# Pairs of squares added on POOL before PE sums them over the features

## The reference

```python
def rms_norm(x, gain=None):
    xf = x.astype(jnp.float32)
    y = xf * lax.rsqrt(jnp.mean(xf * xf, axis=-1, keepdims=True) + RMS_EPS)
...
h = rms_norm(x, norm_g[l, 0]) * (1.0 + sc1) + sh1
```

## Time and profile before

| | us |
|---|---|
| median of 3 runs | 1771.9 (1767.98 to 1773.8) |
| the profiled execution's own time | 1766.4 |
| its span | 1764.4 |
| PE busy | 1561.6 (89%) |
| PE weight loads busy | 1506.8 (85%) |
| DVE busy | 1077.8 (61%) |
| ACT busy | 716.1 (41%) |
| POOL busy | 277.4 (16%) |

### The profile page before, as it was taken

One profiled execution on the slowest core, in us unless ns is written; L12 is line 12 of the kernel. 1 busy time (PEld: TensorE's weight loads), 2 busy tenths in 40 slices (PEclk: granted clock), 3 DMA queues, 4 the chain that ended last, 5 costly groups with the idle time before them and its releaser, 6 DMA issues. The chain is left out here.

```text
span 1764.4 us, 27370 instructions
## 1 busy us (share of the span) xinstructions
PE 1561.6 (89%) x11950; PEld 1506.8 (85%) x11950; DVE 1077.8 (61%) x1279; ACT 716.1 (41%) x797; POOL 277.4 (16%) x221
## 2 busy tenths in 40 slices
PE   2897689999898689999897685999989998899999
PEld 2886589999787589999897584999989997899998
DVE  6765757787455448688474633576895443456444
ACT  2533345433542445533474411433334443343332
POOL 0000200053000001044000111010253700300012
PEclk7998779999798579999798885899998999889999
DMA  9570549787140228888243001378893542436650
GB/s 395 224 262 1 207 187 350 291 332 291 72 160 32 76 92 320 324 308 333 99 170 117 1 1 35 146 281 303 312 354 144 189 173 93 143 129 229 217 211 29
DMA packets 47207, 336.71 MB, mean 191 GB/s; under 512 B 5360, under 2 KB 5744, under 8 KB 6768
## 3 DMA queue, kind: packets, MB, share of 16 engines
q1 hardware_dynamic: 46224, 333.09, 50.7%
q10 hardware_dynamic: 864, 1.87, 0.3%
HBM read 333.89 MB, written 1.05 MB: 190 GB/s over the span
## 5 line engine op out<-in xcount | busy, mean ns | idle before, releaser
L417 DVE TENSOR_TENSOR weights_hi_lo<-ring,weights_hi_lo 128x2048 fp32r<-128x2048 f32 x213 | 514.5, 2417 | 399.2 <-ACT weights_hi_lo L411 398.4
L411 ACT ACTIVATE weights_hi_lo<-ring 128x2048 fp32r<-128x2048 f32 x213 | 407.4, 1914 | 638.8 <-PE PS L519 347.1
L519 PE MATMUL PS<-hi,weights_hi_lo 128*128 128x256 f32 x3200 | 526.9, 288 | 25.5 <-DVE weights_hi_lo L417 17.1
L519 PEld LDWEIGHTS PS<-hi,weights_hi_lo 128*128 128x128 f32 x3200 | 451.3, 195 | 29.4 <-DVE weights_hi_lo L417 19.1
L789 PE MATMUL PS<-acts_hi_lo,weights_hi_lo 128*128 128x256 f32 x3552 | 446.3, 288 | 33.9 <-DVE weights_hi_lo L417 21.1
L789 PEld LDWEIGHTS PS<-acts_hi_lo,weights_hi_lo 128*128 128x128 f32 x3552 | 439.2, 196 | 41.3 <-DVE weights_hi_lo L417 25.0
L519 PE MATMUL PS<-lo,weights_hi_lo 128*128 128x256 f32 x1600 | 326.7, 286 | 0.0
L519 PEld LDWEIGHTS PS<-lo,weights_hi_lo 128*128 128x128 f32 x1600 | 253.8, 195 | 0.0
L428 DVE CUSTOM_DVE_ANT_0 ring<-ring,cond 128x1024 f32<-128x1024 f32 x192 | 248.4, 1333 | 1.0 <-DMA smallS<-in_small_dram 0.9
L737 POOL CAST acts_hi_lo<-arena 128x512 fp32r<-128x512 f32 x74 | 73.8, 998 | 993.6 <-PE PS L789 538.2
L519 PE MATMUL PS<-weights_hi_lo,hi 128*128 128x256 f32 x1248 | 203.2, 284 | 9.2 <-DVE weights_hi_lo L417 8.0
(11 more groups left out here) (325 smaller groups left out, 1100.4 us busy)
## 6 DMA issues: line engine op xcount, KB each, us to landing
ring<-in_stream_dram SPq DMA_DIRECT2D x313, 1024.0 KB, 4.9
constS<-in_const_dram SPq DMA_DIRECT2D x1, 1856.0 KB, 11.3
cond<-in_rows_dram SPq DMA_DIRECT2D x2, 512.0 KB, 6.0
arena<-in_x_dram ACTq DMA_DIRECT2D x1, 1024.0 KB, 12.5
smallS<-in_small_dram SPq DMA_DIRECT2D x1, 883.0 KB, 12.4
out_dram<-arena ACTq DMA_DIRECT2D x2, 256.0 KB, 2.5
out_dram<-arena SPq DMA_DIRECT2D x2, 256.0 KB, 2.9
constS<-in_const_dram SPq DMA_DIRECT2D x1, 320.0 KB, 13.0
```

The source lines that it names most:

```text
L411: act.activation(wsp[:, g % 2, 0, :], ring[:, n % RING, :], ACT.Copy).then_inc(*hi_ready.one())
L417: dve.tensor_tensor(wsp[:, g % 2, 1, :], ring[:, n % RING, :], wsp[:, g % 2, 0, :].bitcast(F32), ALU.subtract).then_inc(used["dve"], 1)
L519: mm = pe.matmul(o, lhs, rhs, start=k + g + j == 0, stop=k == KD - 1 and j == 2, skip_group_check=True)
```

## The change

POOL gets a part in each group of sums (`pair_squares`): for each of the three units of two tiles it waits for the squares and adds the second tile's 256 columns to the first's, in place, in float32. PE (`unit_sums`) waits for that sum in place of the squares, and multiplies only the first 256 columns by the ones: two matmuls for each unit, ten in a group for sixteen. The units of one tile are summed as before. In the start phase and in the output and down projections POOL's part stands behind the work that it had there. New signals `x_squares_paired` and `y_squares_paired` order it. The rest of the diff, left out below, removes signals that no instruction used.

```diff
--- before.py
+++ after.py
@@ -32,6 +32,7 @@
 EARLY_CONST = 266
 MOD_COLS = 40
 UNITS = ((0, 1), (2, 3), (4, 5), (6,), (7,))
+PAIRS = 3
 
 
 IN = {}
@@ -583,13 +584,21 @@
             state["taken"] = [bank_taken(i) for i in range(n_pe)]
             close()
 
-        def unit_sums(pe, u, sq, bank, ready, done):
-
-            pe.wait_ge(*ready.at(u + 1))
-            for c in range(len(UNITS[u])):
-                for m in range(TT):
-                    mm = pe.matmul(PS[:, bank, m:m + 1], sq[:, u % 2, c * SEQ + m * P:c * SEQ + (m + 1) * P], ones[:, 0:1],
-                                   start=u + c + m == 0, stop=u == len(UNITS) - 1, skip_group_check=True)
+        def pair_squares(pool, sq, squared, added):
+
+            for u in range(PAIRS):
+                pool.wait_ge(*squared.at(u + 1))
+                pool.tensor_tensor(sq[:, u % 2, 0:SEQ], sq[:, u % 2, 0:SEQ], sq[:, u % 2, SEQ:2 * SEQ], ALU.add).then_inc(*added.one())
+
+        def unit_sums(pe, u, sq, bank, squared, added, done):
+
+            if u < PAIRS:
+                pe.wait_ge(*added.at(u + 1))
+            else:
+                pe.wait_ge(*squared.at(u + 1))
+            for m in range(TT):
+                mm = pe.matmul(PS[:, bank, m:m + 1], sq[:, u % 2, m * P:(m + 1) * P], ones[:, 0:1],
+                               start=u + m == 0, stop=u == len(UNITS) - 1, skip_group_check=True)
             mm.then_inc(*done.one())
 
         def spread(pe, r, bank, ready, done):
@@ -607,14 +616,14 @@
             sq = area(TEMP_AT, 2, 512)
             tmp, r = spare[:, 0:1024].rearrange("p (i t) -> p i t", i=4), stat[:, 48:50]
             R = PS[:, 2, 0:SEQ]
-            xsq, xsum, xrt, xr, rx, td, hd, ld = (sig(n) for n in (
-                "x_squares", "x_square_sums", "x_roots", "x_rstd", "x_rstd_spread", "x_scaled", "h_hi_ready", "h_lo_ready"))
+            xsq, xad, xsum, xrt, xr, rx, td, hd, ld = (sig(n) for n in (
+                "x_squares", "x_squares_paired", "x_square_sums", "x_roots", "x_rstd", "x_rstd_spread", "x_scaled", "h_hi_ready", "h_lo_ready"))
             state["h_hi"] = [hd.at(k + 1) for k in range(KD)]
             state["h_lo"] = [ld.at(k + 1) for k in range(KD)]
 
             def pe_part(pe):
                 for u in range(len(UNITS)):
-                    unit_sums(pe, u, sq, 0, xsq, xsum)
+                    unit_sums(pe, u, sq, 0, xsq, xad, xsum)
                 spread(pe, r, 2, xr, rx)
 
             def act_part(act):
@@ -645,7 +654,10 @@
                         dve.scalar_tensor_tensor(lo[:, k - 1, :], tmp[:, (k - 1) % 4, :], mods[:, q, k - 1:k],
                                                  hi[:, k - 1, :].bitcast(F32), ALU.add, ALU.subtract).then_inc(*ld.one())
 
-            return pe_part, act_part, dve_part
+            def pool_part(pool):
+                pair_squares(pool, sq, xsq, xad)
+
+            return pe_part, act_part, dve_part, pool_part
 
         def start_phase(blk):
 
@@ -691,6 +703,10 @@
                     if k % 2:
                         mm.then_inc(*tr.one())
                 norm[0](pe)
+
+            @blk.gpsimd
+            def _(pool):
+                norm[3](pool)
 
             @blk.vector
             def _(dve):
@@ -747,8 +763,8 @@
             slots, todo = slots_of(name)
             normed = l < 2
             gate = mod_part(l, half, 2)
-            bd, ysq, ysum, yrt, yr, ry, yg, yt, xu = (sig(n) for n in (
-                "tile_products", "y_squares", "y_square_sums", "y_roots", "y_rstd", "y_rstd_spread", "y_gated", "y_scaled", "x_updated"))
+            bd, ysq, yad, ysum, yrt, yr, ry, yg, yt, xu = (sig(n) for n in (
+                "tile_products", "y_squares", "y_squares_paired", "y_square_sums", "y_roots", "y_rstd", "y_rstd_spread", "y_gated", "y_scaled", "x_updated"))
             following = slots_to_split() if next_norm else []
             norm = norm_of(*next_norm, xu) if next_norm else None
             sq, T, z = area(TEMP_AT, 2, 512), area(TEMP_AT + 1024, 2, 512), area(0, KD, SEQ)
@@ -769,6 +785,10 @@
             @blk.gpsimd
             def _(pool):
                 split_acts(pool, lhs, slots, acts_split, acts_ready)
+                if normed:
+                    pair_squares(pool, sq, ysq, yad)
+                if norm:
+                    norm[3](pool)
 
             @blk.tensor
             def _(pe):
@@ -793,10 +813,10 @@
                             if k < KD - 1:
                                 mm.then_inc(*bd.one())
                             if normed and unit_ends[k]:
-                                unit_sums(pe, unit_ends[k] - 1, sq, 0, ysq, ysum)
+                                unit_sums(pe, unit_ends[k] - 1, sq, 0, ysq, yad, ysum)
                     mm.then_inc(*multiplied.one())
                 if normed:
-                    unit_sums(pe, n_units - 1, sq, 0, ysq, ysum)
+                    unit_sums(pe, n_units - 1, sq, 0, ysq, yad, ysum)
                     spread(pe, r, 3, yr, ry)
                 if norm:
                     norm[0](pe)
...
```

More of the change, by code:

```diff
@@ L971, in short_mixers @@
                 "square_sums", "mean_ready", "root_ready", "outputs_ready", "outputs_turned", "gla_zeroed"))
-            dfr, vn, wm, gt = sig("centred"), sig("gmlp_normed"), sig("ws_masked"), sig("gla_out_taken")
+            dfr, vn, wm = sig("centred"), sig("gmlp_normed"), sig("ws_masked")
             c4 = c.rearrange("p (n t) -> p n t", n=4)
@@ L1203, in nsa_phase @@
             cs, sd, ex, pc = sig("cmp_scores"), sig("cmp_shifted"), sig("cmp_exp"), sig("cmp_probs")
[L1204 to L1207, removed]
+            pct, pcs, oc = (sig(n) for n in ("cmp_probs_T", "cmp_probs_T_taken", "cmp_out"))
+            ws, wt, mxd, pe_, ptp, pts, ob = (sig(n) for n in (
+                "scores_in_psum", "scores_taken", "row_max", "probs_ready", "probs_T_in_psum", "probs_T_taken", "attn_out"))
             gd, fin, ft = sig("gates_ready"), sig("outputs_ready"), sig("outputs_turned")
@@ L1619, in delta_inputs @@
             taken = sig("gemm_bank_taken")
-            tap0, cv, sl, sqd, ss, rt, nr = (sig(n) for n in (
-                "first_tap", "conv_done", "conv_silu", "squares_ready", "l2_sums", "root_ready", "l2_done"))
+            tap0, cv, sl, sqd, ss, rt = (sig(n) for n in (
+                "first_tap", "conv_done", "conv_silu", "squares_ready", "l2_sums", "root_ready"))
             ga, ge, gl, bt = sig("gate_abs"), sig("gate_exp"), sig("gate_log"), sig("beta_ready")
```

## The result

| | us |
|---|---|
| changed kernel, median of 22 runs | 1780.01 (1770.7 to 1788.49) |
| kernel before, median of 22 runs | 1767.82 (1761.13 to 1774.14) |
| ratio | 1.0062, 95% interval 1.0046 to 1.0077 |
| changed kernel's profiled execution: span | 1782.9 (before 1764.4) |

The change costs 0.62% by the ratio, 11.0 us of 1768 (8.1 to 13.6 by the interval); the two medians alone differ by 12.2. The forecast was +5.9 us, slower, at 1777.8 in 1769 to 1786. In the groups of the page (busy us, mean ns of one, idle before) the sums have shrunk as they should, and what waits has changed: PE's idle time before them has doubled and ends with POOL, for ACT in the earlier trace rows.

The account below looks back on a forecast made before the run. PE, busy 89% of the span, was taken as the bound. Start +1.0, projection-output sums +3.4, X sums -1.0 (layers 0, 1) and +2.5 (layers 2, 3) gave +5.9 us: 1772.3 profiled, 1777.8 for the runs' median, range 1769 to 1786.

Parts of the forecast that it names:

- The add: POOL's add of 128x256: 0.74 us free; under a DVE operation with two SBUF inputs it ends 0.59 us after it.
- rival 1: POOL isn't held off by DVE, adds always cost 0.88 us from square to sum: -3.6 us, 1768.3; chance 0.17.
- A: Group of sums over X at the start; first add held behind DVE's split, later squares wait: +1.0 us.
- B: Group of sums over layer 0's output projection; DVE's split ends before its first square: -0.5 us.
- C, E, G, I: Sums over X in layers 0 and 1; PE's saving mostly eaten by adds delayed under DVE: -0.25 us each.
- J: First group of sums over X in layers 2 and 3; adds delay sums, PE at 1.2 GHz: +1.2 us.
- D, F, H: Projection-output sums, layers 0 and 1; PE stands 1.7, 2.3, 1.7 us for adds: +1.07, 1.7, +1.08 us.
- L: Last group of sums over X in layers 2 and 3; same as J: +1.3 us.
- K: Middle group of sums over X in layers 2 and 3; sums stand behind the projection, table load hides the rest: 0.
- rival 3: DVE's L851 and L857, with one PSUM input, hold POOL off too: +12 us in all, 1784; chance 0.12.
- rival 4: The first add, in A, pays for loading POOL's routine, up to the 6.39 us PE waited there: 1784; chance 0.03.
- Rival 2: PE's clock falls to 1.2 GHz in the stalls of D, F, H, 3.1 us each: +9.3, 1787; chance 0.15.

Follow-up runs that it names:

- split_late: Changed kernel with DVE's split of the next slot moved behind the third pair's add of the x-norm; 0.9988 of the kernel before.
- after: First profiled trace of the changed kernel, no further edit; span 1782.9 us, against 1764.4 before.
- again: Changed kernel run and traced a second time, no edit; 1.0063 of the kernel before, +11 us.
- y_only: Changed kernel with only the four y-norms (sums over the projection's output) paired, x-norms summing 16 blocks as before; 1.0057 of the kernel before, +10 us.
- pe_kept_busy: Changed kernel with PE running matmuls nobody reads while it waits for POOL's adds in D, F and H; 1.0025 of the kernel before, +4.4 us.
- before_stalled: Kernel before, no pairing, PE only waiting in D, F and H until DVE has split the next slot; 1.0067 of the kernel before, +11.8 us.

## Why the prediction was right in its steps and short in size

- *The add*, forecast 0.74 us free and 0.59 behind a split: 0.72 to 0.75, and its end 0.58 behind L418 (437.56+2.29 to 440.44). Right, and split_late shows the cause. It also tests a part of rival 1: without the split over the adds the time is 2 us under before, where I had put 3.6 for adds that nothing holds off; in C, E, G and I the adds still lie under DVE's update of X there, at 1.17 us each.
- *A* +1.0: measured +0.80. *B* -0.5: -0.65. *C, E, G, I* -0.25 each: -0.42 each. *J* +1.2: +1.10.
- *D, F, H* +1.07, +1.7, +1.08, with PE standing 1.7, 2.3 and 1.7 us: it stood 1.46, 2.10 and 1.46, and where the clock held the groups grew by 1.0 (after, D), 1.6 (again, F) and 1.03 (y_only, H). Right.
- *L* +1.3: +0.3. I took J's lower clock for L too; in L the last 12 records took 1.78 us, in J 2.72. *K* 0: -0.6 to +0.8, with the clock of the projection under which its first squares lie: 46 of its matmuls took 8.12 us in the trace with +0.8, and 44 took 6.31 in the first.
- *L851 and L857 don't hold POOL off* (rival 3 falls): two adds beside L877 took 1.51 us together in J and in L (timelines of both, J first). *No loading* (rival 4 falls): A's first add starts 0.08 us behind its square, and its 2.38 us end 0.58 behind the split. (The 6.39 us that rival 4 says PE waited there are on no row: the earlier trace rows has 11.23. The bound of 2.68 us for a blocked add is on no row either; the longest took 2.38. The sum uses neither.)

```profile
1134.77 3.22 DVE L877 SCALAR_TENSOR_TENSOR X<-PS,mods,X 128x256 f32<-128x256 f32 x8
...
1136.38 1.51 POOL L591 TENSOR_TENSOR arena<-arena 128x256 f32<-128x256 f32 x2 [9.56 <-ACT arena L635]
...
1139.35 2.72 PE L600 MATMUL PS<-constS,arena 128*128 128x1 f32 x12 [0.80 <-POOL arena L591]
...
1574.99 1.51 POOL L591 TENSOR_TENSOR arena<-arena 128x256 f32<-128x256 f32 x2 [9.57 <-ACT arena L635]
...
1577.96 1.78 PE L600 MATMUL PS<-constS,arena 128*128 128x1 f32 x12 [0.81 <-POOL arena L591]
```

- *The step that was mis-sized is that the rest of D, F and H runs at the same clock*, in the +3.4 us for the y-norms. y_only measured +10 in time, and +5.0 and +3.1 in the groups of its two traces. Rival 2 was no rival but a part of the case: the clock falls in 8 of 18 of these stalls, at 0.9 to 3.6 us in the group. The sum had it at none and the rival at all three, with a chance of 0.15; one or two falls stand only in the upper end of the range. The row that I leaned on, 2.04 us idle without a fall, is a stall in an even stream, and these have one-column sums behind them. No run shows whether that is what makes the difference; the earlier trace rows itself has a fall after 2.52 us.

Some of the nearness is luck. The steps alone, with the clock held and K at 0, add up to +3.5 us in the traces, not to 5.9 (pe_kept_busy, in which nothing falls in D, F and H, has +3.6 in its groups): what was overpriced in L, C, E, G and I covered a part of what the falls cost. And the time of 1777.8 lies so near 1780.0 because its base, 1771.9 from three runs, was 4.1 us above the 1767.8 of 22 runs. The difference of 11.0 us lies outside the +3 to +9 that I gave the forecast case.

Steps and falls give 5.7 to 6.5 us in the traces; the time is 11.0 (8.1 to 13.6). The missing 5 us (2 to 8) lie outside the groups or in falls that come more often than in the traces. They seem to belong to the stalls too: before_stalled has them (+7.1 in its groups, +11.8 in time) and pe_kept_busy has not (+3.6 and +4.4); the intervals are too wide to call that shown. Where they are stays open: the stretch from A to B varies by 9 us from trace to trace among kernels that are alike there, with the clock, and that is more than what is sought. The clock is where I would look first: of the changed kernel's 22 runs the four with a mean granted clock of 0.914 or more took 1774 to 1776 us, the two at 0.899 took 1786.5 and 1787.1. That ties the time to the clock, not the clock to the stalls.

## What to carry to other kernels

Here an add on POOL took 0.72 us alone and 2.38 beside a DVE operation with two SBUF inputs: before moving work there, look for such operations beside it, and move those first. A wait of 1.5 to 2.1 us in the middle of PE's stream cost about its length in its group and, in 8 of the 16 that the traces have, the clock behind it; price it at both, and put it where PE stands anyway. And work saved on the bound engine shows only once its inputs come fast enough: here ten matmuls for sixteen paid once the adds were clear of DVE's split, each unit had its own buffer and PE took a single unit in between; with the first alone the gain could not be told from zero.

## What the hardware showed that I had not expected

Stalls of 0.9, 1.5 and 0.9 us, 3.3 us in all of 1768, cost 11.8 us (7.6 to 16). The changed kernel's stalls are longer, 5.0 us in all; filled with matmuls for nothing they left a loss of 4.4 us (0.9 to 8.0) in place of 11, the x-norms' part included. PE's clock, at 1.2 or 2.4 GHz, fell in some executions and not in others of the same program: behind F's stall in the first and third trace of the changed kernel, not in the second. The spread of the times does not tell the kernels apart: 17.8 us for the changed kernel over 22 runs and 13.0 for the one before, but 17.7 over 12 runs of split_late, in whose trace no clock fell in D, F or H.
